# A hybrid attention and expert layer on one core: three remainders made one stage earlier, and two steps of the attention loops exchanged

## The reference

```python
def mixing_sublayer(h, lw, rope_a, rope_b, ctx):
    z = h @ lw['w_in']
    q_a, k_a, v_a, c_q, c_kv, k_r, g_a, g_b = jnp.split(z, cuts, axis=-1)
    qa = rmsnorm(q_a.reshape(b, s, H_A, HD_A), lw['gqa_qn'])      # A: 8 heads of 128, 2 key heads
    ka = rmsnorm(k_a.reshape(b, s, KV_A, HD_A), lw['gqa_kn'])
    cq = rmsnorm(c_q, lw['mla_qa_g'])
    qb = (cq @ lw['w_qb']).reshape(b, s, H_B, NOPE_B + ROPE_B)    # B: 8 heads of 128 + 64 rotary
    ...
    o_a = block_attention(qa, ka_all, va_all, HD_A ** -0.5)
    kvb = (ckv_all @ lw['w_kvb'])                                 # keys and values of B
    kb_nope = rmsnorm(kvb[..., :NOPE_B], lw['mla_kn_nope'])
    o_b = block_attention(qb_full, kb, vb, (NOPE_B + ROPE_B) ** -0.5)
    merged = jax.nn.sigmoid(g_a) * (o_a @ lw['w_oa']) + jax.nn.sigmoid(g_b) * (o_b @ lw['w_ob'])
    return merged @ lw['w_out'], ctx_out
```

## Time and profile before

| what | value |
|---|---|
| median of 3 runs | 1769.77 us (1768.54 to 1770.4) |
| the profiled execution | 1767.64 us, span 1765.8 us |
| granted clock, mean | 0.954 of full speed |
| PE busy | 1562.3 us, 88% |
| DVE busy | 1007.9 us, 57% |
| ACT busy | 728.2 us, 41% |
| POOL busy | 653.8 us, 37% |
| A, 190 to 300 us | PE busy 7.3 to 10.0 of each 10 us, DVE 6.2 to 8.4 |
| B, 360 to 460 us | PE busy 88.1, DVE 61.4, ACT 35.8, POOL 23.6 of 100 us |

### The profile page before, as it was taken

One profiled execution on the slowest core, in us unless ns is written; L12 is line 12 of the kernel. 1 busy time (PEld: TensorE's weight loads), 2 busy tenths in 40 slices (PEclk: granted clock), 3 DMA queues, 4 the chain that ended last, 5 costly groups with the idle time before them and its releaser, 6 DMA issues. The chain is left out here.

```text
span 1765.8 us, 22716 instructions
## 1 busy us (share of the span) xinstructions
PE 1562.3 (88%) x7699; PEld 1181.3 (67%) x7699; DVE 1007.9 (57%) x1578; ACT 728.2 (41%) x1067; POOL 653.8 (37%) x727
## 2 busy tenths in 40 slices
PE   7799787788889999999892999999999999999990
PEld 2688687688879998964541666666666666666660
DVE  1956677656665466526552666555555555555644
ACT  2423343333342131102212566555565555656650
POOL 0533474422213332310055345444444444444540
PEclk9999899889989999999896999999999999999995
DMA  9320100000015465444163899999999999999944
GB/s 320 96 93 3 37 1 1 1 1 1 1 47 150 139 204 177 135 148 158 72 263 128 290 357 374 351 344 341 345 348 347 339 344 345 342 332 341 339 149 181
DMA packets 129672, 352.50 MB, mean 200 GB/s; under 512 B 21316, under 2 KB 77256, under 8 KB 102600
## 3 DMA queue, kind: packets, MB, share of 16 engines
q1 hardware_dynamic: 97880, 237.71, 36.9%
q10 hardware_dynamic: 10288, 71.86, 11.1%
q0 software_dynamic: 21440, 42.08, 9.5%
HBM read 335.16 MB, written 47.87 MB: 217 GB/s over the span
## 5 line engine op out<-in xcount | busy, mean ns | idle before, releaser
L2247 DVE TENSOR_TENSOR e_wlo<-mem,e_whi 128x2048 fp32r<-128x2048 f32 x140 | 314.6, 2288 | 119.8 <-ACT e_whi L2187 119.8
L2187 ACT ACTIVATE e_whi<-mem 128x2048 fp32r<-128x2048 f32 x140 | 260.3, 1908 | 36.0 <-PEq L1847 23.6
L2157 PE MATMUL psum<-mem 128*128 128x512 f32 x560 | 252.0, 593 | 1.5 <-ACT mem L2219 1.5
L2137 PE MATMUL psum<-e_whi,e_xhi 128*128 128x512 f32 x560 | 228.2, 407 | 7.1 <-DVE e_xlo L2254 7.1
L2094 POOL TENSOR_TENSOR held<-nhalf 1x1 f32<-1x1 f32 x206 | 126.2, 613 | 284.5 <-DMA sums<-mem_h,si 118.6
L2139 PE MATMUL psum<-e_wlo,e_xhi 128*128 128x512 f32 x560 | 222.3, 397 | 0.0
L2138 PE MATMUL psum<-e_whi,e_xlo 128*128 128x512 f32 x560 | 222.2, 397 | 0.0
L2157 PEld LDWEIGHTS psum<-mem 128*128 128x128 f32 x560 | 101.0, 190 | 102.2 <-issue 102.1
L1481 POOL TENSOR_TENSOR w_lo<-mem,w_hi 128x1024 fp32r<-128x1024 f32 x30 | 76.8, 2581 | 161.3 <-ACT w_hi L1425 161.3
L2254 DVE TENSOR_TENSOR e_xlo<-psum,e_xhi 128x512 fp32r<-128x512 f32 x140 | 90.2, 686 | 77.8 <-ACT e_xhi L2193 77.8
L927 ACT ACTIVATE mem<-psum,small 128x640 f32<-128x640 f32 (+1 forms) x80 | 60.3, 754 | 175.6 <-DVE small L1096 107.2
(11 more groups left out here) (313 smaller groups left out, 3309.5 us busy)
## 6 DMA issues: line engine op xcount, KB each, us to landing
mem<-in_w_e SPq DMA_DIRECT2D x144, 1024.0 KB, 12.4
mem<-in_w_e ACTq DMA_DIRECT2D x66, 1024.0 KB, 11.2
mem<-in_w_mod SPq DMA_DIRECT2D x24, 1024.0 KB, 12.5
mem<-in_w_in SPq DMA_DIRECT2D x16, 512.0 KB, 4.5
mem<-in_w_in SPq DMA_DIRECT2D x3, 2048.0 KB, 8.9
sums<-mem SPq DMA_DIRECT2D x10, 512.0 KB, 16.6
mem<-sums SPq DMA_DIRECT2D x10, 512.0 KB, 7.8
mem<-in_x_sample SPq DMA_DIRECT2D x8, 512.0 KB, 11.4
```

Of the source, the lines that this page charges most:

```text
L2137: pe.matmul(out, xh, wh, start=first, stop=False)
L2157: mm = pe.matmul(pY[:, cs], gT[:, f, :], w2[v][:, f, cs], start=(f == 0), stop=(f == 1))
L2187: act.activation(wHi13[u % 2][:, a], w13[u][:, a], ACT.Copy).then_inc(se["h13"], 1)
L2247: dve.tensor_tensor(wLo13[u][:, a], w13[u][:, a], wHi13[u % 2][:, a].bitcast(F32), ALU.subtract)\
```

## The change

It moves `qHiA` and `qLoA` ahead of the projection stage and lets GpSimd make the halves of A's heads 0 and 1 there, behind the powers of units 16 and 17. It makes the halves of B's first key at the end of GpSimd's work in the stage of B's keys. The counts in the waits are lowered to fit. In A, ScalarE copies the transposed slice of tile n-2 ahead of the exponential of tile n, in B still behind it. In B, VectorE takes the remainder of the next head's query ahead of scaling tile t=1, and the mean behind it as before.

```diff
--- before.py
+++ after.py
@@ -350,6 +350,9 @@
         return nc.alloc_sbuf_tensor_at(name, [rows, *shape], F32R, offset=mem_at + 4 * at)
 
 
+    qHiA = [fp32r(f"qa_hi{b}", M_R + 7168 + 640 * b, TOK) for b in range(2)]
+    qLoA = fp32r("qa_lo", M_OA, HA, TOK)
+    s_qs = sem("s_qs")
     kHiA, kLoA = fp32r("ka_hi", M_TB + 3840, KVA, KEYS), fp32r("ka_lo", M_SC + 5696, KVA, KEYS)
     krHH, krLo = fp32r("kr_hi", M_TB + 6912, KEYS), fp32r("kr_lo", M_SC + 7232, KEYS)
     wqb = mem.at(M_SC + 1024, 2, HB * (NOPE + ROPE))
@@ -590,6 +593,14 @@
                 pool.tensor_tensor(zrs[i % 2][:, 0:g], zss[i % 2][:, 0:g], nhalf[:, 0:g], ALU.pow).then_inc(s_zr, 1)
                 if t in AHEAD and c < 3:
                     weights_lo(c + 1, range(*AHEAD[t]))
+                if c == 3 and t in (1, 2):
+
+                    h = t - 1
+                    pool.wait_ge(s_z, 3 * NT)
+                    pool.wait_ge(s_ze, NT)
+                    pool.tensor_copy(qHiA[h][:, :], qT[:, h, :]).then_inc(s_qs, 1)
+                    pool.wait_ge(s_qs, h + 1)
+                    pool.tensor_tensor(qLoA[:, h, :], qT[:, h, :], qHiA[h][:, :].bitcast(F32), ALU.subtract)
 
         @block.vector
         def _(dve):
@@ -821,9 +832,9 @@
                         if h:
                             pe.wait_ge(s["qe"], 2 * h)
                             pe.wait_ge(s["ql"], 2 * h)
-                        pe.wait_ge(s["kl"], h + 1)
-                    elif t == 0:
-                        pe.wait_ge(s["ql"], h + 1)
+                            pe.wait_ge(s["kl"], h)
+                    elif t == 0 and h >= 2:
+                        pe.wait_ge(s["ql"], h - 1)
                     if mla and t == 2:
                         if h + 1 < nh:
                             pe.wait_ge(s["qe"], 2 * h + 1)
@@ -935,9 +946,11 @@
                     act.activation(pT[:, 4, (t - 1) * P:t * P], pT_ps[:, 512:640], ACT.Copy).then_inc(s["TeA"], 1)
 
                 for n in range(N + lag + 1):
+                    if not mla and lag <= n < N + lag and TILES[n - lag][1]:
+                        take_p(n - lag)
                     if n < N:
                         softmax(n)
-                    if lag <= n < N + lag and TILES[n - lag][1]:
+                    if mla and lag <= n < N + lag and TILES[n - lag][1]:
                         take_p(n - lag)
                     if n > lag:
                         h, t = TILES[n - lag - 1]
@@ -969,7 +982,7 @@
                         if h >= 2:
                             pool.wait_ge(s["S"], NT * (h - 1))
                         pool.tensor_copy(kh, kB[:, h, :]).then_inc(s["kh"], 1)
-                        pool.wait_ge(s["kh"], h + 1)
+                        pool.wait_ge(s["kh"], h)
                         pool.tensor_tensor(kl, kB[:, h, :], kh.bitcast(F32), ALU.subtract).then_inc(s["kl"], 1)
 
                     def square(h):
@@ -980,7 +993,6 @@
                         pool.wait_ge(s["ms"], h)
                         pool.tensor_tensor(hrs[h % 2], hss, nhalf[:, 0:NT], ALU.pow).then_inc(s["rs"], 1)
 
-                    keys(0)
                     for h in range(1, nh):
                         keys(h)
                         square(h)
@@ -996,10 +1008,9 @@
                     def split(h):
 
                         qh, ql, _ = q_of(h)
-                        if h >= 2:
-                            pool.wait_ge(s["S"], NT * (h - 1))
+                        pool.wait_ge(s["S"], NT * (h - 1))
                         pool.tensor_copy(qh, qT[:, h, :]).then_inc(s["qh"], 1)
-                        pool.wait_ge(s["qh"], h + 1)
+                        pool.wait_ge(s["qh"], h - 1)
                         pool.tensor_tensor(ql, qT[:, h, :], qh.bitcast(F32), ALU.subtract).then_inc(s["ql"], 1)
 
                     def square(t):
@@ -1026,8 +1037,6 @@
                         pool.wait_ge(s["rx"], 5 * t + 4)
                         pool.tensor_tensor(qrot[:, :, t * ROPE:(t + 1) * ROPE], rc, rr, ALU.add).then_inc(s["rx"], 1)
 
-                    split(0)
-                    split(1)
                     for h in range(1, nh):
                         if h <= NT:
                             square(h - 1)
@@ -1120,11 +1129,12 @@
                     if n >= lag:
                         take_p(n - lag)
                     if n < N:
+                        h, t = TILES[n]
+                        if mla and h + 1 < nh and t == 1:
+                            remainder(h + 1)
                         normalise(n)
-                        h, t = TILES[n]
                         if mla and h + 1 < nh:
                             if t == 1:
-                                remainder(h + 1)
                                 mean(h + 1)
                             if t == 2:
                                 scale(h + 1)
@@ -1137,8 +1147,6 @@
         nc.clear_and_free_semaphores(list(s.values()))
         nc.all_engine_barrier()
 
-    qHiA = [fp32r(f"qa_hi{b}", M_R + 7168 + 640 * b, TOK) for b in range(2)]
-    qLoA = fp32r("qa_lo", M_OA, HA, TOK)
     attend("a", oA, lambda h: (qHiA[h % 2][:, :], qLoA[:, h, :], None),
            lambda h: (kHiA[:, h // (HA // KVA), :], kLoA[:, h // (HA // KVA), :]),
            lambda h: vA[:, :, h // (HA // KVA), :], (M_R + 8448, M_R + 9088, M_R + 6144, M_R))
@@ -1157,7 +1165,7 @@
     kHiB = [fp32r(f"kb_hi{b}", o, KEYS) for b, o in enumerate((M_TB + 6016, M_TB + 8960))]
     kLoB = fp32r("kb_lo", M_R, HB, KEYS)
     names = ("kv", "sq", "ss", "ms", "rs", "kn", "v", "T", "e",
-             "q_Z", "q_c", "q_h", "q_l", "q_sq", "q_ss", "q_ms", "q_rs", "q_iv", "q_n", "q_T", "q_r")
+             "q_Z", "q_c", "q_h", "q_l", "q_sq", "q_ss", "q_ms", "q_rs", "q_iv", "q_n", "q_T", "q_r", "q_k")
     sk = {n: nc.alloc_semaphore(name=f"s_k_{n}") for n in names}
 
     KV = NOPE + VD
@@ -1258,6 +1266,10 @@
             pool.tensor_tensor(hrs[0], hss, nhalf[:, 0:NT], ALU.pow).then_inc(sk["q_rs"], 1)
             for h in range(2, HB):
                 power(h)
+            pool.wait_ge(sk["e"], 1)
+            pool.tensor_copy(kHiB[0][:, :], kB[:, 0, :]).then_inc(sk["q_k"], 1)
+            pool.wait_ge(sk["q_k"], 1)
+            pool.tensor_tensor(kLoB[:, 0, :], kB[:, 0, :], kHiB[0][:, :].bitcast(F32), ALU.subtract)
 
         @block.vector
         def _(dve):
```

## The result

The changed kernel takes 1747.96 us (median of 4 runs, 1747.53 to 1751.16) against 1769.15 us before (4 runs, 1765.75 to 1770.4): a ratio of 0.9884, 95% interval 0.9869 to 0.9898. The forecast was 1749.0 in a range of 1744 to 1757. The profiled execution has a span of 1745.7 us (before 1765.8) and a mean granted clock of 0.964 (before 0.954).

What follows compares the result with a forecast made beforehand. In A, VectorE and ScalarE handing tiles to and fro bound it; in B, TensorE's 11.6 us stall on the remainder mattered. 2.3 - 0.7 + 0.8 + 0.5 + 2.7 + 11.1 + 4.0 = 20.7 us gained; median 1749.0, range 1744 to 1757.

Steps and rivals of the forecast that it cites:

- Start of A: Entry to attention A: with both GpSimd pairs made earlier, TensorE starts when it enters; gain 2.3 us, bounds 1.3 to 2.4.
- Contention: Projection: GpSimd's moved pair stretches VectorE's L659 and L660 by 2.0 us, making transposes 0.7 us late, paid once.
- ScalarE's order in A: Attention A: slice copied ahead of the exponential gains 0.8 us over five rotary heads, plus 0.5 at A's end.
- the 0.56 of the text: Attention A: TensorE's next transposes run 0.56 us earlier, but off the path in most tiles; upper bound 3.9 over seven heads.
- One sign: Attention A: VectorE's wait on scores should become smaller by only as much as the heads gain.
- Start of B: Entry to attention B: key pair made in the stage before at no cost; TensorE starts 2.7 us earlier, bounds 1.7 to 2.8.
- Remainder: Attention B: remainder ahead of t=1's scaling brings scores 1.59 us earlier in seven heads, 11.1 us; bounds 7.6 to 11.6.
- Clock: Attention B: with TensorE's stall before L840 gone, low-clock stretches mostly go too; gain 4.0 us, bounds 0 to 4.7.
- the low clock stays: Rival, B: the clock's falls move to other waits; gain 16.7 us, time 1753.1; chance 0.15.
- the stall changes its owner: Rival, B: ScalarE's rounded query or GpSimd's squares become last; gain 13.2 us, time 1756.6; chance 0.10.
- slower: Rival, A's 32 wide tiles: the copy makes exponentials wait for transposes; 11 us more, 1781; chance 0.03.
- the time after 530 us changes by over 2 us: Refutation sign, behind B: nothing is changed there, so apart from the clock it should move one for one with B's end.

Runs made afterwards that it cites:

- The single-part runs: Kernel before plus only B's remainder ahead of scaling: 1753.14 us, ratio 0.9912; changed kernel with only that exchange taken back: 1761.68 us, ratio 0.9951.
- the filler run: Kernel before plus ten unused 256-column matmuls behind B's sums of squares, keeping TensorE at work in the stall: 1776.7 us against 1781.26, ratio 0.9988.
- the run with `scale` moved: Changed kernel with VectorE's rotary scaling of B's next query moved from behind t=2's scaling to behind t=3's maximum: 1763.01 us, ratio 0.9905.
- two of the runs above: Changed kernel, GpSimd's projection pairs waiting for VectorE's normalised rows: 1756.34 us; changed kernel, B's later key pairs held back and rotary scaling behind t=3's maximum: 1744.75 us.

## Why the prediction was right, and where it was not

**Start of A.** Right in size and cause. TensorE's entry, not shown before, was taken 2.3 us ahead of its old start; by the trace its idling fell from 3.31 to 0.94 us, 2.4 less. Contention lost VectorE 1.8 us (forecast 2.0) and the stretch 0.67 us (forecast 0.7), once and not twice (both pairs stretch VectorE by the same 1.8 us, but only the first makes TensorE wait). The rule of the Trainium skill that was weighed here ("GPSIMD Engine Reference", "8. Key points") held, and spoke for the right sum. Both stretched additions have two inputs in SBUF.

**ScalarE's order in A.** Right in size (1.49 for 1.3), and by its parts too, if they are read where the stage's longest chain runs. Counted from first matmul to first matmul the heads gain 0.56, 0.27, 0.16, 0.16, 0.15, 0.17 and 0, and the end nothing, which looks like two misses that cancel. But there TensorE is ahead of VectorE for a while. In the first head its transposes of tile t=2 come 0.53 us earlier, the 0.56 of the text, and of that only 0.28 is left at the maxima of the second head's later tiles. Counted at ScalarE's last copy of each head's values, the run with this order alone leads the kernel before by 0.27, 0.44, 0.59, 0.74, 0.90, 0.89, 0.98 and 1.46 us, both counted from A's first matmul (189.08 before, 188.99 in that run); the changed kernel's leads are the same within 0.03. The copies of the last two heads and the transposes between, before and, from the third line, in that run:

```profile
295.44 0.59 ACT L949 ACTIVATE mem<-psum 128x512 f32<-128x512 f32 x1
305.39 0.60 ACT L949 ACTIVATE mem<-psum 128x512 f32<-128x512 f32 x1 [1.96 <-PE psum L879]
294.38 0.59 ACT L951 ACTIVATE mem<-psum 128x512 f32<-128x512 f32 x1
296.69 0.74 PE L857 MATMUL psum<-ident,mem 128*128 128x128 f32 x5 [0.24 <-issue]
303.84 0.60 ACT L951 ACTIVATE mem<-psum 128x512 f32<-128x512 f32 x1 [1.96 <-PE psum L879]
```

The five heads with rotary rows brought 0.27 and then 0.17, 0.15, 0.15 and 0.16 us, 0.90 where 0.8 was forecast; the two after them 0.08; and the end 0.48 for 0.5. That last gain comes at the transposes of 298.29, 296.69 here: they are 1.5 us ahead, the scores just before them only 1.0. One sign failed: VectorE's wait on scores fell from 11.9 to 7.2 us, by more than A gained.

**Start of B.** 2.73 for 2.7. The pair at the end of the keys' stage cost nothing that shows.

**Remainder.** 1.59 us a head were forecast, and 20.90 - 19.31 = 1.59 came, in six heads; the first kept 0.5 us of the wait, and ran partly at the low clock. The single-part runs show it as the cause: with the stall B takes 172.2 to 174.3 us in four traces, without it 158.4 to 159.4 in the five that leave `scale` and ScalarE's order in B where they were.

**Clock.** Forecast 4.0 with bounds 0 and 4.7. B's 15.6 less 11.1 leaves 4.5, and the filler run, which keeps the stall and takes only the clock's fall away, gives 4.9, a little above the upper bound. That bound counted one late maximum a head and nothing else that a low stretch may delay, and it was read from one execution. The four traces with the stall have 5, 4, 5 and 7 low stretches between the stage's start and its last head, 21 in all, most 3.4 us long, in other heads each time, and B's length varies by 2.1 us with them. So the size of this term is in part a draw of each execution, a reading that the text set aside because three totals lay close together; that it came out near 4.0 owes something to which execution was profiled. Its cause isn't a draw: all 21 begin during the stall before `L840` or within 1.6 us of its end, and the ten traces in which TensorE doesn't idle there have none between the first head and the last. The rival *the low clock stays* had 0.15; other waits of TensorE remained in the heads, up to 0.67 us in the changed kernel and 2.28 in the run with `scale` moved, and the clock didn't fall at them. The rival *the stall changes its owner* holds for the first head alone, as was said; *slower* is refuted by A's length: the 21.4 us for which ScalarE now waits ahead of its slice were idle before too, under another name.

**Behind B.** The text said it would be wrong "if the time after 530 us changes by over 2 us", and by the two profiled executions it did: the merge starts 23.1 us earlier, the end comes 20.1 us earlier. The stretch behind the merge's start is 1232.2 us before and 1235.2 after. It isn't the change: in the six other traces of the quicker chips it is 1234.2 to 1238.0, whichever part of the change they hold, so the profiled execution of before is the odd one, and its total lies 1.5 us under its median. The other way round, 1.5 of the 23.1 us stood at 160 us already, ahead of the first changed instruction. The near hit of the total, 1.0 us off, owes something to these two: the forecast of the changed stretch was 0.9 us short (20.7 for 21.6), and the rest is what two executions of one kernel differ by. What makes the stretch behind B vary wasn't tried.

## What to carry to other kernels

In an in-order queue, look at what stands ahead of a small result that another engine waits for: one exchange on VectorE gave over two thirds of this gain, and the other three moves the rest. Price a recurring stall of TensorE with the clock it can cost, here 3 to 5 us on top of its own 11, and take that price from more than one trace. Compare two engines' gains where the longest chain runs, not where one of them is ahead for a while. When work of GpSimd is moved into an idle stretch, look at what VectorE does there, down to its smallest instructions, and tie it by a semaphore to a point where VectorE reads PSUM or waits, as in two of the runs above.

## What the runs showed of the hardware

- A VectorE product of 128x1 took 1.77 us in place of 0.16 when it began 0.05 us behind a GpSimd subtraction of 128x768, and 0.16 again once the subtraction had moved; a small instruction isn't spared. In the changed kernel the same happens once, at the start of B (1.60 us at 342.84, beside a subtraction of 1.81), without a cost that shows: TensorE goes on from the projection to the next scores at 345.39 without a wait.
- Contention goes both ways: GpSimd's rounding took 0.93 and its subtraction 1.89 us beside VectorE's two-input additions, 0.72 and 1.56 apart from them.
- Seven stalls of TensorE in B (the first up to 2.3 us, the others 1.55, behind one-column sums of 1.17 us at full clock) went with four to seven falls of the clock to 1.2 GHz in each of four executions, 3.4 us long but for one of 6.8; ten matmuls of no use in each stall (1.44 us) kept it at 2.4 GHz from 352.5 to 520 us. Waits of 2.28 us in front of six heads, in the run with `scale` moved, brought no fall.
